# First block's attention scores as three fp32r products of high and low parts, with the turned blocks copied ahead of a step's probabilities

## The reference

```python
logits = (jnp.einsum('bhqd,bhkd->bhqk', qb, k).astype(jnp.float32) * scale
          + cb[..., :, None] - cum_logf[..., None, :])            # fox
logits = jnp.einsum('bhmqd,bhmkd->bhmqk', qb, k).astype(jnp.float32) * scale   # diff
_, sel = lax.top_k(score, topk)                                   # dsa: 128 kept keys
logits = jnp.einsum('bhqd,bqjd->bhqj', qb, kg).astype(jnp.float32) * scale
p = jax.nn.softmax(jnp.where(valid[:, None], logits, -jnp.inf), axis=-1).astype(vg.dtype)
```

## Time and profile before

| | |
|---|---|
| median of 3 runs | 2403.13 us (2402.93 to 2406.48) |
| profiled execution | 2404.68 us, of it span 2403.0 us |
| PE busy | 2280.4 us (95%) |
| DVE busy | 1279.4 us (53%) |
| ACT busy | 926.8 us (39%) |
| mean granted TensorE clock | 0.977 |
| the chain that ended last | PE 81%, DVE 11%, ACT 3%, issue 3% |
| stage `CausalPairs`, layer 0 and layer 1 | about 156.0 to 300.5 us and 853.4 to 1002.4 us |

### The profile page before, as it was taken

How to read it: one execution, slowest core, us unless ns; L and a number is a source line. 1 busy time by engine, 2 the same in 40 slices (tenths; PEclk the granted TensorE clock), 3 DMA queues, 4 the chain that set the end, 5 groups by cost and what they waited for, 6 DMA issues and landing times.

```text
span 2403.0 us, 32270 instructions
## 1 busy us (share of the span) xinstructions
PE 2280.4 (95%) x13137; PEld 1851.5 (77%) x13137; DVE 1279.4 (53%) x1864; ACT 926.8 (39%) x1555; POOL 261.9 (11%) x167
## 2 busy tenths in 40 slices
PE   6998999999999998899999999998999989998988
PEld 6776678888888765688888878896676878887776
DVE  5678348873225677359853155225555363126764
ACT  3446642222224355642222232324544242115653
POOL 2001112121001011122121000000000000001220
PEclk9999999999999998999999999999999999999999
DMA  5210015632333200035522311321000124223311
GB/s 153 90 60 1 1 53 192 195 121 88 105 97 102 63 35 1 19 123 176 190 91 89 121 63 50 104 78 47 17 12 14 56 71 138 70 70 56 61 30 53
DMA packets 144612, 189.48 MB, mean 79 GB/s; under 512 B 41141, under 2 KB 94402, under 8 KB 144450
## 3 DMA queue, kind: packets, MB, share of 16 engines
q1 hardware_dynamic: 108816, 168.26, 21.5%
q10 hardware_dynamic: 35586, 19.01, 3.5%
q0 software_dynamic: 64, 0.16, 0.0%
HBM read 179.94 MB, written 7.47 MB: 78 GB/s over the span
## 4 chain that ended last, share of the span: by engine, by line
PE 81%; DVE 11%; issue 3%; ACT 3%; ACTq 1%; POOL 0%; DMA 0%; DVEq 0%; POOLq 0%
PE ps L487 63%; PE ps L1720 3%; PE ps L2257 2%; PE ps L1759 2%; DVE ps L1911 2%; PE ps L1724 2%; DVE score L2143 1%; DVE probs_t L1941 1%; PE ps L1773 1%; DVE top L2140 1%; PE ps L2286 1%; PE ps L2274 1%; PE ps L675 1%; ACT probs L1825 1%; DVE sink_part L1901 1%
## 5 line engine op out<-in xcount | busy, mean ns | idle before, releaser
L463 DVE TENSOR_TENSOR w_low<-w_raw,w_high 128x2048 fp32r<-128x2048 f32 (+4 forms) x140 | 305.3, 2181 | 519.6 <-ACT w_high L458 519.6
L458 ACT ACTIVATE w_high<-w_raw 128x2048 fp32r<-128x2048 f32 (+4 forms) x140 | 253.0, 1807 | 631.3 <-PE ps L487 616.9
L487 PE MATMUL ps<-h_hi,w_high 128*128 128x512 f32 x976 | 372.3, 381 | 3.4 <-DVE h_lo L2634 3.2
L487 PE MATMUL ps<-h_lo,w_high 128*128 128x512 f32 x976 | 369.8, 379 | 0.0
L487 PE MATMUL ps<-h_hi,w_low 128*128 128x512 f32 x976 | 369.6, 379 | 0.0
L487 PE MATMUL ps<-w_high,h_hi 128*128 128x512 f32 (+3 forms) x736 | 277.8, 377 | 9.3 <-DVE w_low L463 5.9
L487 PE MATMUL ps<-w_low,h_hi 128*128 128x512 f32 (+3 forms) x736 | 274.8, 373 | 0.0
L487 PE MATMUL ps<-w_high,h_lo 128*128 128x512 f32 (+3 forms) x736 | 274.7, 373 | 0.0
L487 PEld LDWEIGHTS ps<-h_hi,w_high 128*128 128x128 f32 x976 | 184.2, 189 | 38.6 <-issue 4.1
L487 PEld LDWEIGHTS ps<-h_hi,w_low 128*128 128x128 f32 x976 | 184.0, 189 | 34.9
L487 PEld LDWEIGHTS ps<-h_lo,w_high 128*128 128x128 f32 x976 | 184.3, 189 | 34.2 <-issue 0.5
(11 more groups left out here) (324 smaller groups left out, 3724.9 us busy)
## 6 DMA issues: line engine op xcount, KB each, us to landing
w_raw<-in_w_gate_up SPq DMA_DIRECT2D x44, 1024.0 KB, 5.2
ada_w<-in_ada_w SPq DMA_DIRECT2D x24, 1024.0 KB, 5.2
w_raw<-in_w_down SPq DMA_DIRECT2D x20, 1024.0 KB, 4.9
w_raw<-in_w_in SPq DMA_DIRECT2D x16, 1024.0 KB, 5.1
w_raw<-in_c_in_w SPq DMA_DIRECT2D x16, 1024.0 KB, 5.5
w_raw<-in_w_out SPq DMA_DIRECT2D x8, 1024.0 KB, 4.8
w_raw<-in_ab_in_w SPq DMA_DIRECT2D x8, 1024.0 KB, 5.1
bias<-bias_scratch ACTq DMA_DIRECT2D x32, 224.0 KB, 5.1
```

The lines of the kernel that those rows point to most:

```text
L458: e.activation(w_high[j % 2][:, 0:size], w_raw[j % 2][:, 0:size], ACT.Copy).then_inc(sig.w_high_done, 1)
L463: e.tensor_tensor(w_low[j % 2][:, 0:size], w_raw[j % 2][:, 0:size], w_high[j % 2][:, 0:size].bitcast(F32), ALU.subtract).then_inc(sig.w_lo ...
L487: mm = e.matmul(dst, lhs, rhs, start=start and a == 0, stop=stop and a == 2)
```

## The change

Queries and keys are split in a high part (fp32r, what ACT copies into `q_turned`, `k_turned`, `kd_turned`) and a low part (fp32r), which DVE computes as the transposed block in PSUM less the high part. The low parts are written over the columns of `proj` that were turned (`proj_low`, and `keys_low` over `keys_twice`), and `o_diff` moves to columns no longer needed. `scores` then adds three fp32r products for each map, high by high, high by low and low by high, with both maps next to each other in each of the three. `qk_ready` now comes from DVE (`low_turned`) and a new signal `qk_high` from ACT. PE does a turn, and ACT its copy, ahead of `turn_probs(s)` and `copy_probs(s)`. DVE's loop begins at -4 for the low parts, with its rounds at the same steps as before.

```diff
-        o_diff = proj[:, 0:2, DQ:DQ + 512]
-        o_diff_sq = proj[:, 2:4, DQ:DQ + 512]
-        q_turned = [at(f"q_turned{i}", [P, S], F32, W0 + 24576 + 2048 * i) for i in range(2)]
-        k_turned = [at(f"k_turned{i}", [P, S], F32, W0 + 28672 + 2048 * i) for i in range(2)]
-        kd_turned = at("kd_turned", [P, S], F32, W0 + 40960)
+        o_diff = proj[:, 0:2, FQ:FQ + 512]
+        o_diff_sq = proj[:, 2:4, FQ:FQ + 512]
+        q_turned = [at(f"q_turned{i}", [P, S], F32R, W0 + 24576 + 2048 * i) for i in range(2)]
+        k_turned = [at(f"k_turned{i}", [P, S], F32R, W0 + 28672 + 2048 * i) for i in range(2)]
+        proj_low = at("proj_low", [P, NT, IN_W], F32R, R + 32768)
+        keys_low = at("keys_low", [P, NT, P], F32R, W0 + 43008)
+        kd_turned = at("kd_turned", [P, S], F32R, W0 + 40960)
...
-                self.units, self.turns, self.first_turn = [], [], []
-                col = lambda c: (lambda t: proj[:, t, c:c + P])
+                self.units, self.turns, self.first_turn, self.lows, self.group_of = [], [], [], [], []
+                col = lambda c: (lambda t: proj[:, t, c:c + P], proj_low[:, :, c:c + P])
...
-                for c, (which, src) in enumerate(chunks):
+                self.lows.append({})
+                for c, (which, (src, low)) in enumerate(chunks):
+                    self.lows[g][which] = low
                     dst = {"q": q_turned[g % 2], "k": k_turned[g % 2], "d": kd_turned}[which]
-                    self.turns.append((first - self.AHEAD - len(chunks) + c, dst, src, g))
+                    self.turns.append((first - self.AHEAD - len(chunks) + c, dst, src, low))
+                    self.group_of.append(g)
...
-                    q, k = q_turned[x.group % 2], kd_turned if x.kind == "dsa" else k_turned[x.group % 2]
-                    for m in range(2):
-                        e.matmul(ps[:, self.bank(s, m), 0:n], q[x.rows(m), t * P:n], k[x.rows(m), 0:n], start=True, stop=False)
+                    tiles = lambda a: a[:].rearrange("p (b c) -> p b c", c=P)
+                    q, k = tiles(q_turned[x.group % 2]), tiles(kd_turned if x.kind == "dsa" else k_turned[x.group % 2])
+                    q_low = self.lows[x.group]["q"]
+                    k_low = self.lows[5]["d"] if x.kind == "dsa" else self.lows[x.group]["k"]
+                    for a, (qs, ks) in enumerate(((q, k), (q, k_low), (q_low, k))):
+                        for m in range(2):
+                            e.matmul(ps[:, self.bank(s, m), 0:n].rearrange("p (b c) -> p b c", c=P), qs[x.rows(m), t, :],
+                                     ks[x.rows(m), 0:t + 1, :], start=a == 0, stop=False)
...
                     if 0 <= s + self.AHEAD < self.N:
                         scores(s + self.AHEAD)
+                    if s in self.mid:
+                        turn(self.mid[s])
                     if 0 <= s < self.N:
                         turn_probs(s)
-                    if s in self.mid:
-                        turn(self.mid[s])
...
-                    e.activation(dst[:], ps[:, 7, :], ACT.Copy).then_inc(sig.qk_ready, 1)
+                    e.activation(dst[:], ps[:, 7, :], ACT.Copy).then_inc(sig.qk_high, 1)
...
+                    if s in self.mid:
+                        copy_turned(self.mid[s])
                     if 0 <= s < self.N:
                         copy_probs(s)
-                    if s in self.mid:
-                        copy_turned(self.mid[s])
...
+                def low_turned(i):
+                    _, dst, _, low = self.turns[i]
+                    e.wait_ge(sig.qk_high, B["qk_high"] + i + 1)
+                    tiles = lambda a: a.rearrange("p (b c) -> p b c", c=P)
+                    e.tensor_tensor(low, tiles(ps[:, 7, :]), tiles(dst[:].bitcast(F32)), ALU.subtract).then_inc(sig.qk_ready, 1)
+
                 done, rounds = 0, 3 * ROUNDS
-                for s in range(-2, self.N):
-                    if s + self.AHEAD < self.N:
+                for s in range(-4, self.N):
+                    if 0 <= s + self.AHEAD < self.N:
                         maxima(s + self.AHEAD)
+                    if s in self.mid:
+                        low_turned(self.mid[s])
                     if (s + 2) % NT == 0 and s > 0:
                         invert((s + 2) // NT - 1)
-                    share = min(rounds, rounds * (s + 3) // self.ROUND_STEPS)
+                    share = min(rounds, rounds * max(0, s + 3) // self.ROUND_STEPS)
```

6 lines of the change are left out of this document (3 added, 3 removed).

## The result

The changed kernel takes 2430.17 us (median of 6 runs, 2419.57 to 2436.32), the kernel before beside it 2406.19 us (6 runs, 2402.93 to 2407.49). The ratio is 1.0101 (95% interval 1.0085 to 1.0117): 24 us slower, with an interval clear of no change. The forecast was 2411.6 us with a range up to 2421. The direction was right, the size was not, and the time lies outside the range.

What follows compares the result with a forecast made beforehand. DVE was taken to set or share the pace up to the keep mask, PE after it. Mask delays 3.3 + 1.8, start 4.2 and -0.8 behind the mask gave +8.5 us: 2411.6 us, range 2401 to 2421.

Steps and rivals of the forecast that it cites:

- Products, -4.8: Score products on PE: three fp32r products save 0.24 us a unit, -4.8 us over 20 units (-2 to -8.6).
- The lower bound's 0.43 a unit: Score products: largest saving for a unit of four steps, from three times n / 2.4 GHz and not under 0.11 us.
- the bound of -8.6: Score products: far end of the saving, 20 units at 0.43 us each, if PE sets the pace in all.
- the third rival: PE sets the pace throughout and gets its full saving: -5.8 us, 2397.3 us, faster; chance 0.06.
- The rule of the Trainium skill that was set aside: Small products on PE: some 60 cycles overhead per matmul; 128-column step about 0.37 us, another -2.6 us in all.
- Low parts' duration, 0.60 of the queue each: DVE: each low part takes 0.68 us, costing 0.60 us of queue; ten a layer before the keep mask, 6.0 us.
- Start, +4.2: Start of both stages: first scores wait for `w_low` and two low parts in series, +2.1 us a layer (sum 2.8 to 4.2).
- Delay of the mask, +3.3 and +1.8: Up to the keep mask: low parts on DVE, partly hidden in its waits for PE, delay it in layers 0 and 1.
- Behind the mask, -0.8: After the keep mask: three units save 0.7 us, two group changes cost 0.17 each; -0.4 a layer (sum -2 to 0).
- Move at no cost: Turns and ACT's copies ahead of the step's probabilities: same copies in another order, where PE has time to lose; 0 us.
- The sum, +8.5: Whole kernel: 3.3 + 1.8 + 4.2 - 0.8 us, giving 2411.6 us against the median of 2403.13.
- The clock, rival at 0.16: Both stages: clock falls more often, two more half-clock stretches where PE sets the pace, +7 us, 2418.6 us; chance 0.16.

Runs made afterwards that it cites:

- e1: Kernel before with three fp32r products of the high parts for each map in place of the fp32 one, no low parts: 2401.0 us.
- e8: Changed kernel with the first group's keys turned in bank 6 instead of bank 7 behind the queries' low part: 2420.01 us.
- e11: Kernel before with three fp32r products and four low parts a layer for the sparse heads (steps 28 to 39) only: 2412.65 us.
- e3: Kernel before with only the turns and ACT's copies moved ahead of the step's probabilities: 2409.71 us.
- e5: Changed kernel with the turns and ACT's copies back in the old order, behind the step's transposes and copies: 2426.06 us.
- e4: Changed kernel with low parts made but unused: scores wait for ACT's copies and all three products take high parts: 2421.7 us.
- e14: Changed kernel with every low part computed twice on DVE, one after the other: 2457.26 us.
- e13: e8 with eight useless 512-column products on PE between the second turn and the stage's first scores: 2425.5 us.
- e2: Changed kernel with fp32 products and the old order of turns; low parts made and waited for but not used: 2429.61 us.
- e6: Changed kernel with six useless 512-column products behind each of the first two turns and ahead of each later group's first scores: 2432.48 us.
- e7: e6 with two more useless products ahead of the scores of every other step from 3 to 27: 2426.87 us.
- e9: e8 with eight useless products between the second turn and first scores, and three ahead of each later group's first scores: 2418.63 us.
- e10: e8 with ten low parts a layer made by GpSimd from a second, plain ACT copy instead of by DVE: 2428.41 us.

## Why the prediction was wrong

- **Products, -4.8:** right. -5.7 at equal half clock (e1); steps of 0.90 and 0.48 us at 512 and 128 columns, forecast 0.90 and 0.54, of which 0.06 was taken off afterwards. In e1's profile the two first parts are together 3.2 us shorter (94.0 and 96.5 us) at about the same half clock, so that DVE alone did not set the pace there. (The lower bound's 0.43 a unit is a slip: three times n / 2.4 GHz, not under 0.11, gives some 0.3 to 0.4. It touches the bound of -8.6 and the third rival alone.) The rule of the Trainium skill that was set aside in the prediction (TensorEngine Tiling, Instruction Overhead) would have given 0.37 us for the step at 128 columns, an estimate from its 60 cycles; the trace has 0.48.
- **Low parts' duration, 0.60 of the queue each:** right (0.68 to 0.69 us each, DVE busy 6.6 and 6.1 us longer up to the mask).
- **Start, +4.2:** nearly right, 2.5 + 2.3 us, by the chain that was drawn up; e8 takes 3.6 of it away.
- **Delay of the mask, +3.3 and +1.8:** this is the step that failed. In the profiled executions, counted from the first scores, it is +12.4 and +7.5 us (94.9 to 107.4, 98.8 to 106.3). The step asked how much of 6.7 us disappears in DVE's waits for PE, and left the clock as it was. The 19.9 us go with 45 us more at half clock between the first scores and the masks (87 against 42 us), which at 0.31 make some 14 us; the 6 us left are about the 5.1 forecast. Its picture of DVE from 197 us to the mask as an engine that never waits for PE did not hold either: it waits 6.6 us there.
- **Behind the mask, -0.8:** wrong by 2 us. The part is 1.0 and 0.1 us longer, and in e11 2.2 and 0.4. Some 1.2 us of it go with 4 us more at half clock. In e1, without low parts, it is 0.5 and 2.6 us shorter, so that the low parts' share looks larger than the 0.7 us forecast for their changes of group; these are single executions.
- **Move at no cost:** wrong by itself (e3, +3.2); inside the change it is made good at equal half clock, but not in the median (e5).
- **The sum, +8.5:** at equal half clock the changed kernel lies 9.0 us above before. The sum was about right for a clock that stays. That is partly luck: the scores' waits for low parts cost 6.9 (by e4), and DVE's work with the move and the start 7.8, and the sum had mixed them.
- **The clock, rival at 0.16:** it was the one that counted, and it was priced at 7 us, two stretches of 6.9 us. Measured: 47 us more of half clock, and 0.31 x 47 = 15 us. In the profiled executions nearly all of it lies in the two stages. The sign that the prediction had named for this, half-clock stretches before the mask that double, came: from the first turns to the masks it is 93 us, where it was 42. The reason given against it, that before the mask much is hidden because DVE is still busy 5.6 of 6.9 us, took one row for the rule: at 206.5 to 230.4 us PE is busy 99% and DVE 71%. The rule of the Trainium skill beside it (TensorE: Matmul & The Clock Gate, HAM oscillation), idle between groups of matmuls costs the full clock, points the right way as far as more waits of PE went with more half clock (e14, 181 us against 157); e13 shows that filling one such idle moment is not enough.

What is shown: making the low parts on DVE, with the waits for them, makes the loss (e2 against before, e14), and more time at half clock goes with it; more work on PE gives the clock back (e6, e7, e9). What stays open: which of PE's idle moments let the clock fall. The scores' waits for low parts alone are not it (e4, 155 us without them, though PE then waits more for the probabilities and the mask), nor is the start alone (e13). Filling all of them takes back 36 of the 47 us (e6), but a fill is also work on PE, so the runs do not tell the gaps from PE's share of work. And the 0.31 us is a slope between executions, not a clock that was set; how e10 loses 4.9 us at equal half clock against e8 was not taken apart. None of the versions beats the kernel before; the only one that cannot be told from it, e1, leaves the low parts out.

## What to carry to other kernels

Read the mean clock of each run beside its time before explaining a difference: here some 15 of 24 us went with the clock. In a stage where two engines share the pace, a step that lengthens the way between them can cost by its wait and once more by the clock, as here, even if the engine that does the step has idle time on its page. Price such a rival by what the clock already does in that stage (42 us at half clock there before), not by one stretch.

## What the runs showed of the hardware

- The same kernel spends 131 to 175 us at half clock from one execution to the next, and takes 2419.57 to 2436.32 us with it; a single profile is one draw.
- Doubling the low parts on DVE raised the mean time at half clock from 157 to 181 us, and two useless products on PE ahead of most steps brought it to 72 us. That less work on PE by itself costs clock is not shown: with the products alone it is 120 us (standard error 6), against 110.
- After 1.7 us of useless products in the idle start of the stage the clock still fell, to 0.59 over the next 20 us (0.57 without them).
- Pairs of fp32r products on 32 rows of the array, 128 columns each, follow one another after 204.16 - 204.05 = 0.11 us, the floor that was assumed for small products.
